# Gated MLP of a two-network kernel: V half first, its norm and mixing between the U slabs

## The reference, cut to what matters

```python
def gmlp_chunk_mix(h, w_uv, v_norm, w_s, b_s, w_o):
    B, S, _ = h.shape                       # 1, 256
    z = jax.nn.gelu(h @ w_uv)               # 1024 -> 4096
    u, v = jnp.split(z, 2, axis=-1)         # 2048 each
    v = rms_norm(v, v_norm)                 # over the 2048 features
    v = v.reshape(B, S // GMLP_CHUNK, GMLP_CHUNK, GMLP_GROUPS, GMLP_GROUP_DIM)  # 2 chunks, 16 groups of 128
    causal = jnp.tril(jnp.ones((GMLP_CHUNK, GMLP_CHUNK), dtype=bool))
    ws = jnp.where(causal[None], w_s, jnp.zeros_like(w_s))
    sv = jnp.einsum('gts,bcsgd->bctgd', ws, v) + jnp.transpose(b_s)[:, :, None]
    sv = sv.reshape(B, S, GMLP_WIDTH)
    return (u * sv) @ w_o                   # 2048 -> 1024
```

## Time and profile before

| what | value |
|---|---|
| runs, median of 3 | 2755.38 us (2748.97 to 2791.28) |
| the profiled execution's own time | 2775.27 us |
| its span in the trace | 2773.3 us |
| mean granted TensorE clock | 0.971 |
| TensorE busy | 2622.9 us, 95% |
| VectorE busy | 1754.8 us, 63% |
| ScalarE busy | 1310.3 us, 47% |
| GpSimd busy | 74.8 us, 3% |
| read from HBM | 421.12 MB, 152 GB/s over the span |
| chain that ended last | PE 85%, DVE 5%, ACT 4%, issue 4%, DMA 1% |

### The profile page before, as it was taken

How to read it: one execution, slowest core, us unless ns; L and a number is a source line. 1 busy time by engine, 2 the same in 40 slices (tenths; PEclk the granted TensorE clock), 3 DMA queues, 4 the chain that set the end, 5 groups by cost and what they waited for, 6 DMA issues and landing times.

```text
span 2773.3 us, 60909 instructions
## 1 busy us (share of the span) xinstructions
PE 2622.9 (95%) x23330; PEld 2545.7 (92%) x23330; DVE 1754.8 (63%) x2815; ACT 1310.3 (47%) x1934; POOL 74.8 (3%) x106
## 2 busy tenths in 40 slices
PE   7998998999999998899989998699999999999999
PEld 7996877989999997789989998589999999999999
DVE  5757665667657655567757656857667566555674
ACT  5544343455445444345545445345455454454552
POOL 0000441000000000000000000000000000000000
PEclk9999998999999999799999999999999999999999
DMA  5553201435555555145654644125545564552564
GB/s 196 201 184 110 92 3 47 160 129 182 194 170 197 191 178 169 46 144 180 208 172 160 208 158 164 54 86 197 197 166 191 189 176 129 137 138 99 163 208 144
DMA packets 114315, 424.16 MB, mean 153 GB/s; under 512 B 12433, under 2 KB 19044, under 8 KB 113796
## 3 DMA queue, kind: packets, MB, share of 16 engines
q1 hardware_dynamic: 105696, 408.99, 44.3%
q10 hardware_dynamic: 8484, 13.30, 2.3%
HBM read 421.12 MB, written 1.12 MB: 152 GB/s over the span
## 4 chain that ended last, share of the span: by engine, by line
PE 85%; DVE 5%; ACT 4%; issue 4%; DMA 1%; ACTq 0%; DVEq 0%; POOL 0%; SPq 0%; POOLq 0%
PE bank L455 20%; PE bank L456 20%; PE bank L457 20%; PE bank L389 4%; PE bank L390 3%; PE bank L391 3%; ACT hi L339 2%; PE bank L2102 2%; PE bank L1521 1%; PE bank L1496 1%; PE bank L436 1%; PE bank L437 1%; PE bank L438 1%; PE bank L1505 1%; PE bank L2030 1%
## 5 line engine op out<-in xcount | busy, mean ns | idle before, releaser
L347 DVE TENSOR_TENSOR lo<-raw,hi 128x1024 fp32r<-128x1024 f32 (+1 forms) x728 | 936.0, 1294 | 456.8 <-ACT hi L339 455.7
L455 PE MATMUL bank<-Hh,hi 128*128 128x256 f32 x3360 | 942.7, 281 | 24.0 <-DVE lo L347 22.2
L339 ACT ACTIVATE hi<-raw 128x1024 fp32r<-128x1024 f32 (+1 forms) x728 | 787.0, 1106 | 328.1 <-PE bank L391 155.2
L456 PE MATMUL bank<-Hl,hi 128*128 128x256 f32 x3360 | 938.8, 279 | 0.0
L457 PE MATMUL bank<-Hh,lo 128*128 128x256 f32 x3360 | 938.8, 279 | 0.0
L455 PEld LDWEIGHTS bank<-Hh,hi 128*128 128x128 f32 x3360 | 637.8, 190 | 30.8 <-DVE lo L347 30.2
L456 PEld LDWEIGHTS bank<-Hl,hi 128*128 128x128 f32 x3360 | 638.0, 190 | 0.0
L457 PEld LDWEIGHTS bank<-Hh,lo 128*128 128x128 f32 x3360 | 634.9, 189 | 0.0
L455 PE MATMUL bank<-Ah,hi 128*128 128x256 f32 x1408 | 392.3, 279 | 0.0
L457 PE MATMUL bank<-Ah,lo 128*128 128x256 f32 x1408 | 392.3, 279 | 0.0
L456 PE MATMUL bank<-Al,hi 128*128 128x256 f32 x1408 | 392.2, 279 | 0.0
(11 more groups left out here) (411 smaller groups left out, 3943.3 us busy)
## 6 DMA issues: line engine op xcount, KB each, us to landing
raw<-in_w SPq DMA_DIRECT2D x600, 512.0 KB, 3.4
raw<-in_w SPq DMA_DIRECT2D x128, 704.0 KB, 4.2
dB<-dil_bias ACTq DMA_DIRECT2D x16, 384.0 KB, 9.7
X<-in_x SPq DMA_DIRECT2D x2, 512.0 KB, 5.4
mem_x<-in_mem ACTq DMA_DIRECT2D x1, 1024.0 KB, 5.1
gWS<-in_ws ACTq DMA_DIRECT2D x1, 1024.0 KB
gBS<-in_bs ACTq DMA_DIRECT2D x1, 1024.0 KB
out_x<-X SPq DMA_DIRECT2D x4, 256.0 KB, 2.6
```

The costliest lines, as they stand in the source:

```text
L339: act.activation(k.hi[:, q, :w], k.raw[:, q, :w], ACT.Copy).then_inc(k.hi_ready, 1)
L347: dve.tensor_tensor(k.lo[:, q, :w], k.raw[:, q, :w], k.hi[:, q, :w].bitcast(F32), ALU.subtract).then_inc(k.lo_ready, 1)
L455: pe.matmul(out, wh, xh, start=first, stop=False)
L456: pe.matmul(out, wh, xl, start=False, stop=False)
```

## The change

All of it is in the gated MLP and in three helpers.

- SP loads the slabs of the second half of `gmlp_uv` (V) first, then those of the first half (U). Slab numbers, buffers and waits stay as they were.
- `pe_first_stage` with `pair=True` ends after the first two slabs; the rest is written out slab by slab instead of in loops, on all three engines.
- On ScalarE each slab's high half now stands ahead of the Gelu. In the V phase a square of the slab follows; VectorE adds it to a running sum `gSS`. TensorE sums over partitions with one product, behind the first U slab.
- ScalarE loads Sqrt's table, takes the root and loads Gelu's table again in iteration 1 of U. VectorE writes the reciprocal to its own tile `gRV`, since `R` is still in use.
- V's scalings, transposes, copies and mixing products stand between the U slabs, two banks each (5 and 6, 7 and 4). In iteration u of U, TensorE does slab 16+u, transposes pair u-3 and mixes pair u-5; VectorE scales pair u-2, adds the bias of pair u-6, and takes the products with U for the pairs that `PRODUCTS` names (pairs 0 to 5 in iterations 6 to 11, pair 6 in 13, pair 7 in 15), their low halves an iteration later.
- VectorE waits for and masks the mixing weights in iteration 8 of V.
- The tiles move: V comes first in `gVU`, `gGh` takes V's place and `gGl` that of the transposed V.

```diff
@@ sp_stage
+        if st.name == "gmlp_uv":
+            half = st.iters // 2
+            with sp.Fori(0, half) as i:
+                body(i, RING * half)
+            with sp.Fori(half, st.iters) as i:
+                body(i, -RING * half)
+            return
@@ pe_stage
         elif after_first:
             first_pair(None if late else after_first)
+            if pair:
+                return
             body(0, 2)
@@ GatedMlp.pe
+        sh.pe_first_stage(pe, self.uv, pair=True)
+        def slab(s):
+            sh.pe_slab(pe, self.uv.base + s, k.bank[s % RING], lambda kc: (k.Hh[:, kc, :], k.Hl[:, kc, :]), spare=RING)
+        def square_sum():
+            k.dve_done.wait(pe, f"g.add{G - 1}")
+            pe.wait_ge(k.rstd_ready, sh.norm_n["pe"])
+            k.pe_done.done(pe.matmul(k.bank[4][:, :T], k.ones, self.SS[:], start=True, stop=True), "g.ss")
+        def turn(b):
             k.dve_done.wait(pe, f"g.vn{2 * b + 1}")
+            if b >= 2:
+                k.act_done.wait(pe, f"g.vt{b - 2}")
...
+        def mix(b):
             k.act_done.wait(pe, f"g.vt{b}")
+            if b >= 2:
+                k.dve_done.wait(pe, f"g.sv{b - 2}")
...
+        for s in range(2, G):
+            slab(s)
+        for u in range(G):
+            slab(G + u)
+            if u == 0:
+                square_sum()
+            if 0 <= u - 3 < 8:
+                turn(u - 3)
+            if 0 <= u - 5 < 8:
+                mix(u - 5)
@@ GatedMlp.act
+        def high(s):
+            s += st.base
+            sh.act_hi(act, s + RING, s % RING, 8, s // RING + 1)
+        def gelu(s):
+            act.wait_ge(k.banks_freed, RING + st.base + s + 1)
+            act.activation(self.VU[:, s, :], self.TMP[:, s % RING, :], ACT.Gelu_apprx_tanh).then_inc(k.gelu_done, 1)
+        def square(s):
+            act.wait_ge(k.gelu_done, RING + s + 1)
+            if s >= 2:
+                k.dve_done.wait(act, f"g.add{s - 2}")
+            k.act_done.done(act.activation(self.SQ[:, s % 2, :], self.V[:, s, :], ACT.Square), f"g.sq{s}")
+        def deviation():
+            act.preload_act_table(ACT.Sqrt)
+            k.pe_done.wait(act, "g.ss")
+            k.act_done.done(act.activation(k.STD[:], k.bank[4][:, :T], ACT.Sqrt, bias=k.col(C_EPS), scale=1.0 / (2 * D)), "g.std")
+            act.preload_act_table(ACT.Gelu_apprx_tanh)
...
+        for s in range(G):
+            high(s)
+            gelu(s)
+            square(s)
+        for u in range(G):
+            high(G + u)
+            if u == 1:
+                deviation()
+            gelu(G + u)
+            if 0 <= u - 4 < 8:
+                turned(u - 4)
+            for b in self.PRODUCTS.get(u - 1, ()):
+                product(b)
...
+    PRODUCTS = {6 + b if b < 6 else 2 * b + 1: (b,) for b in range(8)}
@@ GatedMlp.dve
+        def slab(s):
+            dve.wait_ge(k.slab_used, st.base + s + 1)
+            dve.wait_ge(k.gelu_done, s + 1)
+            dve.tensor_tensor(self.TMP[:, s % RING, :], k.bank[s % RING][:, :T], k.R[:], ALU.mult).then_inc(k.banks_freed, 1)
+            sh.dve_lo(dve, st.base + s + RING, s % RING, 8)
+        def add(s):
+            k.act_done.wait(dve, f"g.sq{s}")
+            if s:
+                k.dve_done.wait(dve, f"g.add{s - 1}")
+                ins = dve.tensor_tensor(self.SS[:], self.SS[:], self.SQ[:, s % 2, :], ALU.add)
+            else:
+                ins = dve.tensor_copy(self.SS[:], self.SQ[:, 0, :])
+            k.dve_done.done(ins, f"g.add{s}")
...
+        for s in range(G):
+            slab(s)
+            if s:
+                add(s - 1)
+            if s == 8:
+                dve.wait_ge(k.mixer_loads, self.loads)
+                k.dve_done.done(dve.tensor_tensor(self.WS[:], self.WS[:], bcast(k.mask("causal"), G), ALU.mult), "g.ws")
+        add(G - 1)
+        for u in range(G):
+            slab(G + u)
+            if u == 1:
+                k.act_done.wait(dve, "g.std")
+                k.dve_done.done(dve.reciprocal(self.RV[:], k.STD[:]), "g.r")
+                k.dve_done.wait(dve, "g.r")
+            if 0 <= u - 2 < 8:
+                scale(2 * (u - 2))
+                scale(2 * (u - 2) + 1)
+            if 0 <= u - 6 < 8:
+                mixed(u - 6)
+            for b in self.PRODUCTS.get(u, ()):
+                product(b)
+            for b in self.PRODUCTS.get(u - 1, ()):
+                low(b)
+        low(7)
```

More of the change, by code:

```diff
@@ L415, in act_stage, with pe_stage @@
         run(act, st, body, between)
-    def pe_stage(self, pe, st, moving, ready, between=None, after_first=None, late=False, rest=False, chunks_first=False):
+    def pe_stage(self, pe, st, moving, ready, between=None, after_first=None, late=False, rest=False, chunks_first=False, pair=False):
         k = self.k
@@ L925, in __init__ @@
+        self.T2 = k.at("gT2", a + 72 * KB, [P, 2, 2, T])
+        self.SS = k.at("gSS", 32 * KB, [P, T])
+        self.RV = k.at("gRV", 33 * KB, [P, T])
         self.loads = 32 + k.loads_before
         k.loads_before += 32
-    def low(self, g, n):
-        return self.Gl[:, g:g + n, :] if g < 12 else self.Gl2[:, g - 12:g - 12 + n, :]
     def pe(self, pe):
         sh, k, G = self.sh, self.k, self.G
[L934 to L942, removed]
+        sh.pe_first_stage(pe, self.uv, pair=True)
@@ L969, in act @@
         sh.norm(act, "act", ACT.Gelu_apprx_tanh)
[L971 to L980, removed]
@@ L985, in act, with turned, product @@
+        def turned(b):
             k.pe_done.wait(act, f"g.vt{b}")
             out = self.VT[:, 4 * b:4 * b + 4, :].rearrange("p a d -> p (a d)")
-            k.act_done.done(act.activation(out, k.bank[b % 4][:], ACT.Copy), f"g.vt{b}")
-        for b in range(8):
+            k.act_done.done(act.activation(out, k.bank[5 + b % 2][:], ACT.Copy), f"g.vt{b}")
+        def product(b):
             k.dve_done.wait(act, f"g.usv{b}")
             k.act_done.done(act.activation(self.Gh[:, 2 * b:2 * b + 2, :], self.U[:, 2 * b:2 * b + 2, :], ACT.Copy), f"g.gh{b}")
+        for s in range(G):
+            high(s)
+            gelu(s)
+            square(s)
@@ L993, in dve @@
     def dve(self, dve):
[L994 removed]
+        sh, k, st, G = self.sh, self.k, self.uv, self.G
         sh.norm(dve, "dve")
[L996 to L1000 removed]
@@ L1001, in dve @@
-        k.act_done.wait(dve, "g.std")
-        k.dve_done.done(dve.reciprocal(k.R[:], k.STD[:]), "g.r")
-        k.dve_done.wait(dve, "g.r")
-        for g in range(self.G):
+        dve.wait_ge(k.rstd_ready, sh.norm_n["dve"])
+        def slab(s):
[3 more added lines that the diff above has]
+            sh.dve_lo(dve, st.base + s + RING, s % RING, 8)
@@ L1007, in dve, with mixed @@
-        for b in range(8):
+            k.dve_done.done(dve.scalar_tensor_tensor(v, v, k.v1("v_norm", g), self.RV[:], ALU.mult, ALU.mult), f"g.vn{g}")
+        def mixed(b):
             k.pe_done.wait(dve, f"g.sv{b}")
-            ps = k.bank[4 + b % 4][:].rearrange("p (g c t) -> p g c t", g=2, c=2)
+            ps = k.bank[(7, 4)[b % 2]][:].rearrange("p (g c t) -> p g c t", g=2, c=2)
             bs = self.BS[:, 2 * b:2 * b + 2, :].unsqueeze(2).broadcast_to([P, 2, 2, P])
```

65 lines of the change are left out of this document (27 added, 38 removed).

## The result

The changed kernel takes 2724.72 us, the median of four runs (2708.67 to 2737.34); the kernel before in the same comparison takes 2760.94 us (2748.97 to 2791.28). The ratio is 0.9845, with a 95% interval from 0.9807 to 0.9884: faster by 1.5%, inside the forecast range of 2678 to 2736 us and within the 2% that the forecast held slightly likelier than more. The two medians lie 36 us apart; by the ratio it is 43. The profiled execution took 2737.34 us, 37.9 us less than the profiled one of before.

What follows compares the result with a forecast made beforehand. Bound: TensorE, losing time in the gated MLP to a ScalarE-VectorE ring, a serial chain and output waits. Products, norm, transposes, mixing and waits sum to 147.7 us, plus 1 for clock: 148.7 against 202.7, so 2701 us; range 2678 to 2736.

Steps and rivals of the forecast that it cites:

- The ring: UV slabs: ScalarE and VectorE wait on each other in turn, 3.09 us a slab; opened, a slab takes 2.77 us.
- the open chain: After UV: sum of squares, norm, 16 scalings, 32 transposes and 32 mixing products run in series with no slab beside them.
- The third part: Output stage: its products wait for each group of gated values to be split; predicted hidden with 0.3 us to spare.
- The products' own time: All 48 slabs of the block: 1152 products at 0.1156 us, 133.1 us (130.5 to 135.7).
- Last square: TensorE's sum of squares waits for the last V slab's addition, some 0.5 us beyond the slab that covers it.
- first transposes: TensorE's wait for the first two scaled V groups, delayed by ScalarE's table loads: about 2.1 us.
- bias adds: U phase: VectorE falls behind, so a bias add that TensorE's mixing waits for comes late; 0.4 us taken.
- Transposes and mixing: Between U slabs, both on TensorE's path: 32 transposes 3.3 us, 64 mixing records 7.3 us.
- The lower clock behind a pause: After a pause of 1 to 2 us TensorE may run at 1.2 GHz: 0 to 3 us, 1 taken.
- The rival of a block at 1.2 GHz: Waits inside U slabs' turns keep TensorE at 1.2 GHz through the block: 2814 us in full; chance 0.03.
- VectorE as the bound: Rival: VectorE bounds the U phase, iterations 6 to 11 at 4.3 to 5.1 us against 4.1; 2710 us, chance 0.17.
- the spacing as a rival: Product spacing changes in stages outside the block: 2725 us if slower, 2670 if faster; chance 0.16, to both sides alike.

Runs made afterwards that it cites:

- the unrolled one: Changed kernel with TensorE's loops over groups of four slabs written out in all stages; block 149.8 us, ratio 0.9795.
- the scalings ahead: Changed kernel with VectorE scaling V groups 0 and 1 right behind the reciprocal, ahead of slab 18's work; block 144.6 and 145.9 us, ratios 0.9801 and 0.9785.

## Why the prediction was right, point by point

- **What bounded the kernel.** Right in all three parts. The ring was shown by the edit of two instructions on ScalarE, made alone (182.4 us) and undone alone (181.8), the open chain by the version without interleaving. The third part, the output products' waits for gated values, had no run of its own; they were 4.3 us in the kernel before and are gone in the changed one.
- **The products' own time.** 133.1 us at the middle of two spacings; the profiled block had the fast one in V and the slow one in the output stage. The two profiles of it, 148.4 and 149.8 us, and the unrolled one, 149.8, stand around the forecast 148.7.
- **Waits.** Last square 0.6 (0.5), first transposes 2.3 (2.1), bias adds none (0.4). Transposes and mixing lie on TensorE's path, as predicted: it was busy for 36.2 of 36.3 us there. The 32 transposes took 3.4 us (3.3; 32 times the row's 0.10 is 3.2), the 64 mixing records 6.5 (7.3).
- **The lower clock behind a pause.** 1 us was taken between 0 and 3. It was 0 in both profiles of the changed kernel and 1.6 to 1.7 us in two of the runs that had the same pause of 2.1 to 2.3 us. Where the pause was taken away (both runs with the scalings ahead) it did not appear. The rival of a block at 1.2 GHz never came near: under 4 us at the lower level were the most in any run that kept the interleaving and the order.
- **VectorE as the bound.** Did not happen; iterations of 4.25 to 4.68 us beside 4.1 were absorbed. With 0.69 us more work a pair TensorE lost 2.2 us, so VectorE was close to being the bound, and the chance of 0.17 was not too high.
- **From the block to the whole time.** The term that was mis-sized, and one of the prediction's own signs of being wrong (148 us in the block, and the whole time does not follow) came in part. The forecast took 54 us off the median, for 2701; measured were 2724.7, inside the wide range of 2678 to 2736 and outside the 2693 to 2712 of the case's own. The ratio of 0.9845 is 43 us, 32 to 53 by its interval; over more rounds 0.9829, 47 us, 32 to 63. Two things explain it. The block of before that the sum was made against, 202.7 us, was a long one: the second profile had 197.6, and against the mean of the two the gain is 51 us. And the rest varies by up to 35 us between executions, through the spacing and, ahead of the block, through the granted clock. I had the spacing as a rival with 0.16 of chance, and other stages' clock not at all; both are no rivals to the forecast but a part of every measurement, and belonged into the range of the case itself. (That rival's fast side is also slightly off: 860 us by the ratio of the two spacings give 33 us, not 34.) 51 us lies inside both intervals. On which side of the 2% line the result fell was near to even in the forecast, 0.52 against 0.45, and with this spread it is in part luck that the likelier side came.

## What to carry to other kernels

When two engines hand one slab back and forth, look at which instruction of a queue really needs the other engine: here the high half never needed the scaling, and standing behind the Gelu it closed a ring of 3.09 us around 2.7 us of products. Open such a ring before interleaving a serial chain between the slabs: one addition inside the closed ring made its turn 3.33 us instead of 3.09. And when a kernel's whole time varies by more than the effect, measure the stage in the profile from one fixed instruction to another, and compare the rest separately, what lies ahead of the stage apart from what lies behind it: here the time that seemed to be lost behind the change was lost ahead of it.

## What the runs showed of the hardware that was not expected

- TensorE's products of 128 x 256 follow one another at 0.1133 or at 0.1178 us with the granted clock at 1.00 in both, in 40 us 355 or 342. A whole feed-forward takes 180.2 or 187.0 us by it. The value turns over at the norm's products near a stage's start (in 121 of 121 places that can be read), sometimes also at a step of 0.28 us ahead of slab 4, and so differs between executions of one program.
- A pause of 2.1 to 2.3 us in an otherwise full stream was followed by the lower clock in two of five profiles that had it (17 products at 0.21 us in one), and cost 1.6 to 1.7 us each time.
- An activation starts 1.29 to 1.30 us after a table load starts, with nothing between, in both directions between Gelu and Sqrt.
